# Neighbourhood value matmuls with the whole 128-column chunk stationary

## What is computed

```python
s_loc = jnp.einsum('bqhd,biqjhd->bhqij', q_row, k_win) * scale + jnp.transpose(bias, (0, 2, 1, 3))[None]
s_ctx = jnp.einsum('bqhd,bkhd->bhqk', q_row, k_ctx) * scale
s = jnp.concatenate([s_loc.reshape(B, H, GRID_W, kh * kw), s_ctx], axis=-1)
p = jax.nn.softmax(s.astype(jnp.float32), axis=-1).astype(v.dtype)
out = (jnp.einsum('bhqij,biqjhd->bqhd', p_loc, v_win)
       + jnp.einsum('bhqk,bkhd->bqhd', p[..., kh * kw:], v_ctx))
```

## Time and profile before

| | |
|---|---|
| median of 3 runs | 1832.72 us (1831.17 to 1834.37) |
| the profiled execution's own time | 1831.06 us |
| its span, first to last instruction | 1829.5 us |
| mean granted TensorE clock | 0.968 |
| neighbourhood stage, first transpose of `sc` to the last value matmul | about 1233.4 to 1402 us of the span |

### The profile page before, as it was taken

One profiled execution on the slowest core, in us unless ns is written; L12 is line 12 of the kernel. 1 busy time (PEld: TensorE's weight loads), 2 busy tenths in 40 slices (PEclk: granted clock), 3 DMA queues, 4 the chain that ended last, 5 costly groups with the idle time before them and its releaser, 6 DMA issues.

```text
span 1829.5 us, 23170 instructions
## 1 busy us (share of the span) xinstructions
PE 1733.7 (95%) x9122; PEld 1465.1 (80%) x9122; DVE 981.4 (54%) x1236; ACT 607.0 (33%) x786; POOL 462.5 (25%) x327
## 2 busy tenths in 40 slices
PE   7999999998977799999998999989999899999998
PEld 7888888788866688888887788878777688888887
DVE  4355544756257678355335545427886545434543
ACT  4243432334242222222223233215665333223330
POOL 3000000000019999899600000015663000000000
PEclk8999999999998899999989899988999899999999
DMA  8312134234224334665422112331100323343332
GB/s 256 92 47 70 47 92 138 93 116 161 70 70 138 92 115 147 186 199 173 135 62 86 47 47 70 101 117 31 48 28 24 92 69 92 90 113 84 94 93 77
DMA packets 227579, 178.48 MB, mean 98 GB/s; under 512 B 5971, under 2 KB 217278, under 8 KB 227502
## 3 DMA queue, kind: packets, MB, share of 16 engines
q1 hardware_dynamic: 218206, 142.74, 26.3%
q0 software_dynamic: 8576, 32.23, 5.3%
q10 hardware_dynamic: 720, 2.41, 0.4%
HBM read 171.37 MB, written 9.13 MB: 99 GB/s over the span
## 4 chain that ended last, share of the span: by engine, by line
PE 80%; DVE 7%; POOL 6%; ACT 3%; issue 3%; DMA 1%; DVEq 0%; ACTq 0%; POOLq 0%
PE ps L1374 25%; PE ps L1376 24%; PE ps L1375 24%; DVE w_lo L870 2%; POOL mod_tmp L1846 2%; POOL sc L1911 2%; POOL mod_tmp L1850 1%; PE ps L1511 1%; PE ps L1753 1%; ACT w_hi L530 1%; PE ps L1448 1%; PE ps L1680 1%; POOL mod_tmp L1852 1%; PE ps L1783 1%; ACT vt_h L803 0%
## 5 line engine op out<-in xcount | busy, mean ns | idle before, releaser
L1374 PE MATMUL ps<-h_hi,w_hi 128*128 128x512 f32 x1376 | 543.7, 395 | 16.3 <-DVE h_lo L879 9.7
L1376 PE MATMUL ps<-h_hi,w_lo 128*128 128x512 f32 x1376 | 539.5, 392 | 0.0
L1375 PE MATMUL ps<-h_lo,w_hi 128*128 128x512 f32 x1376 | 539.3, 392 | 0.0
L870 DVE TENSOR_TENSOR w_lo<-w_raw,w_hi 128x2048 fp32r<-128x2048 f32 (+1 forms) x136 | 343.3, 2524 | 109.1 <-ACT w_hi L530 109.0
L1374 PEld LDWEIGHTS ps<-h_hi,w_hi 128*128 128x128 f32 x1376 | 260.9, 190 | 74.3 <-DVE h_lo L879 9.3
L530 ACT ACTIVATE w_hi<-w_raw 128x2048 fp32r<-128x2048 f32 (+1 forms) x136 | 242.5, 1783 | 188.6 <-PE ps L1376 160.6
L1376 PEld LDWEIGHTS ps<-h_hi,w_lo 128*128 128x128 f32 x1376 | 260.4, 189 | 55.6
L1375 PEld LDWEIGHTS ps<-h_lo,w_hi 128*128 128x128 f32 x1376 | 260.7, 189 | 52.6
L1842 POOL DMA_DIRECT2D mod_raw<-in_l_w_mod x24 | 22.0, 916 | 517.8 <-DVE h_lo L879 505.7
L1374 PE MATMUL ps<-a_hi,w_hi 128*128 128x512 f32 x352 | 138.6, 394 | 0.9 <-DVE w_lo L870 0.9
L1375 PE MATMUL ps<-a_lo,w_hi 128*128 128x512 f32 x352 | 138.0, 392 | 0.0
(11 more groups left out here) (284 smaller groups left out, 2789.2 us busy)
## 6 DMA issues: line engine op xcount, KB each, us to landing
mod_raw<-in_l_w_mod POOLq DMA_DIRECT2D x24, 1024.0 KB, 5.8
w_raw<-in_w_ffn_in SPq DMA_DIRECT2D x44, 512.0 KB, 5.1
w_raw<-in_l_ffn_w_up SPq DMA_DIRECT2D x44, 512.0 KB, 4.9
w_raw<-in_w_in SPq DMA_DIRECT2D x40, 512.0 KB, 5.1
w_raw<-in_l_na_w_qkv SPq DMA_DIRECT2D x24, 512.0 KB, 4.5
w_raw<-in_w_mem_kv SPq DMA_DIRECT2D x16, 512.0 KB, 3.9
w_raw<-in_w_ffn_out SPq DMA_DIRECT2D x16, 384.0 KB, 3.5
w_raw<-in_l_ffn_w_down SPq DMA_DIRECT2D x16, 384.0 KB, 3.6
```

The lines of the kernel that those rows point to most:

```text
L870: v.tensor_tensor(wlo[s][:, 0:size], raw[s][:, 0:size], whi[s][:, 0:size].bitcast(F32), ALU.subtract).then_inc(w_lo, 1)
L1374: mm(o, w_h, x_h, start=first, stop=False, **kw)
L1375: mm(o, w_h, x_l, start=False, stop=False, **kw)
L1376: return mm(o, w_l, x_h, start=False, stop=last, **kw)
```

## The change

In `na_values` the slice of the stationary operand to the head's 64 columns is dropped: all 128 columns of the chunk are loaded, and the output is all 128 partitions of bank 6. Each head's product thus also makes 64 partitions that belong to no one (the weights of this head by the values of its neighbour). The two readouts now read the 64 partitions of their own head. The number of instructions, their order and all waits are unchanged.

```diff
@@ na_out on ScalarE, L805
                 rows = slice(64 * half, 64 * half + 64)
                 act.activation(q_hi[rows, at(a), :].rearrange("p o (r t c) -> p (o t) r c", t=4, c=16),
-                               bank(6)[0:64, :].rearrange("p (t r c) -> p t r c", t=4, r=8), ACT.Copy).then_inc(no_hi, 1)
+                               bank(6)[rows, :].rearrange("p (t r c) -> p t r c", t=4, r=8), ACT.Copy).then_inc(no_hi, 1)
@@ na_out on VectorE, L1277
-                                bank(6)[0:64, :].rearrange("p (t r c) -> p t r c", t=4, r=8),
+                                bank(6)[rows, :].rearrange("p (t r c) -> p t r c", t=4, r=8),
@@ na_values on TensorE, L1756
-                a, cols = head // 2, slice(64 * (head % 2), 64 * (head % 2) + 64)
+                a = head // 2
@@
                 for c in range(4):
                     chunk = 2 * tau + c if c < 2 else 6 + c
-                    last = product(bank(6)[0:64, tau * P:tau * P + P], vt_h[a % 2][:, chunk, cols], vt_l[a % 2][:, chunk, cols],
+                    last = product(bank(6)[:, tau * P:tau * P + P], vt_h[a % 2][:, chunk, :], vt_l[a % 2][:, chunk, :],
                                    np_hi[:, g % 2, c * P:c * P + P], np_lo[:, g % 2, c * P:c * P + P], c == 0, c == 3)
```

## The result

| | before | after |
|---|---|---|
| first measurement, median | 1833.55 us (1831.17 to 1834.64, 4 executions) | 1897.33 us (1886.06 to 2009.76, 4 executions) |
| ratio to before | | 1.0329, 95% interval 1.0268 to 1.0390 |
| profiled execution: time, span, mean granted clock | 1831.06, 1829.5, 0.968 | 1891.51, 1889.9, 0.950 |

The change makes the kernel slower by 3.3%, and the time scatters as the one before does not. The ratio leaves out the execution at 2009.76 us; since what moves the executions apart is the very effect at issue, I list all ten that the changed kernel had in the end: 1870.95, 1886.06, 1891.51, 1903.15, 1983.76, 2009.76, 2011.77, 2012.97, 2013.06 and 2013.07 us. Their median is 1996.8 us, 9% above the kernel before, so the 3.3% of the first measurement comes from the quicker ones.

What follows compares the result with a forecast made beforehand. The neighbourhood stage was taken as bound by PE's instruction list with a few waits. Eight pairs at 4.19 us add 33.5 to the median 1832.72, giving 1866.2 us, 1.018 times before; range 1857 to 1877.

Steps and rivals of the forecast that it cites:

- The load sets the distance: Value matmuls: the 128-column weight load outlasts the matmul, distance 0.06 to 0.112 us, each block 0.63 us longer.
- The readouts cost nothing either way: Readouts of L809: the odd heads' changed partitions cost or gain 0, within 3 ns.
- The waits, step by step: One pair's eight steps: part of the block growth falls into present waits, 20.89 to 25.08 us, growth 4.19.
- st = 5: Sixth step of a pair, counted from 0: new 0.42 us readout wait, 2.74 to 3.79 us.
- slack swallowed: Rival on a pair's steps: all present waits used up, no new one, 3.1 us a pair, 1857 us; chance 0.12.
- waits kept: Rival on a pair's steps: waits stay and distances are 0.12, 6.0 us a pair, 1881 us; chance 0.10.
- Eight pairs, 33.5 us: Whole neighbourhood stage: eight pairs of heads at 4.19 us growth each make 33.5 us.
- The edges: Stage's half-clock head, three blocks, -1.6 to +2.0 us, taken as 0; last four steps' growth may shrink, at most 4 times 0.3.
- 2 us of uncertainty: Outside the stage: granted clock may fall or rise some us sooner or later behind the shifted stage, counted as 2 us.
- quick wide load: Rival on the vt_h and vt_l loads: wide as quick as narrow, distance stays 0.06, 1832.7 us; chance 0.04.
- partly hidden one: Rival on the wide load: distance 0.085 us, block grows 0.30, 1.8 us a pair, 1847 us; chance 0.03.

Runs made afterwards that it cites:

- w2_after: Changed kernel plus unread extra matmuls in TensorE's gaps ahead of the stage, 29 in the second gap: 1861.26 to 1866.47 us in four executions, 2011.95 in one.
- w2_before: Kernel before plus unread extra matmuls in TensorE's gaps ahead of the stage, 29 in the second gap: 1829.13 us, 0.9975 of before.
- again_after: Changed kernel run again with no edit: 1870.95, 1983.76 and four times 2012 to 2013 us.
- gap_wide: Changed kernel with narrow loads for the first pair of heads and a TensorE hole made in the fifth pair: 1929.59 to 1936.18 us.
- w_before: Kernel before plus 39 unread matmuls in TensorE's gaps at the head of the stage, 16 in the second gap: 1829.51 us, 0.9979 of before.

## Why the prediction was wrong, point by point

- **The load sets the distance** (0.112 us, block + 0.63). Right. Distances 0.11, block 1.40 against 0.77. Of the parts, the first distance came out shorter than I put down (0.17 us, not 0.22) and the last one, from the last value matmul to the next transposes, longer (0.12, 1345.74 to 1345.86, against 0.05 to 0.06).
- **The readouts cost nothing either way.** Right: the profile after has 590 to 593 ns for L809, in place of 589 to 592.
- **The waits, step by step.** Right. Forecast for the steps of a pair 2.86, 3.33, 6.23, 2.86, 3.79, 3.12 and 2.89, 25.08 in all; measured 2.86, 3.30, 6.18, 2.83, 3.69, 3.07 and 2.82, 24.75, so that a pair grew by 3.86 and not 4.19. The new wait in st = 5 came, and the waits for POOL went, as put down. Both rivals on the waits (slack swallowed, waits kept) are out.
- **Eight pairs, 33.5 us.** Right as the price of the loads, and some 3 us too high: 30.8 us between the stages of w2_after and w2_before, where both keep the full clock, as eight times 3.86 makes it.
- **The edges.** This is the step that failed. I took from the trace of before that "three blocks run in it" and let them cost -1.6 to +2.0 us in all. The bound for one block was sound, 1.2 us against 1.28 measured (2.62 less 1.34 for the narrow one). What was wrong is the number three. The length of the stretch at half clock was copied from a kernel whose blocks stream without a break there, into one whose blocks don't: 13 blocks in the profiled execution, all 64 in again_after's, and the "2 us of uncertainty" for the clock should have been up to 150. The rows to see it by were there: at half clock the narrow distance was 0.11 us, bound by the array, and I wrote that it might double. A doubled distance means an array that idles half of the time in just those blocks that stand where the clock used to come back, and I did not ask what that does to the clock.
- **The other rivals.** The quick wide load and the partly hidden one are out (0.11 us at full clock). The Trainium skill's fast weight load, which "TensorE: Matmul & The Clock Gate", section "Weight-path perf modes — Fast Weight Load (FWL) and DoubleRow", ties to 128 weights of a type that is not FP32, did not appear in `vt_h`'s fp32r loads: median 192 ns, close to the mean of 189 of the 128-column loads in the earlier trace rows.

What stays open: why one execution of w2_after took 2012 us although its gaps ahead of the stage were filled, what it is in the wide blocks that keeps the clock down, and what decides whether the changed kernel's clock comes back after 30, 90 or 360 us. Nor was a kernel tried in which the wide loads have more than 128 moving columns beside them.

Of the versions run, w2_before beats both kernels, if only just: narrow loads and the unread matmuls ahead of the stage, 1829.13 us, 0.9975 of before (0.9959 to 0.9991). The stretch at half clock ahead of the stage is gone in it:

```profile
1225.00:1236.00 11.00, 11.00 (x57) 8.89 (x56) 5.46 (x18) 2.51 (x6) 5.41 (x7) 1.00 0.55 194
```

## What to carry to other kernels

Where few columns move per weight load (128 here), the width of the stationary operand is time: columns that nobody reads cost as much as real ones. When a change makes matmuls load-bound (their distance is set by the weight load and not by the columns that move), ask also what they do at half clock, and whether a stretch at half clock now in the trace still ends. An estimate that takes the length of such a stretch from the kernel before holds only as long as the work in it stays the same.

## What the runs showed of the hardware

- The clock has memory. The same wide blocks ran at full clock for 81 us and at half clock for 153.6 us in one execution, on either side of a 5.75 us hole. The distances of wide and narrow matmuls stand two to one at full clock (0.11 us against 0.06) as at half clock (0.213 against 0.107), and yet the clock stayed at 1.00 for 192.5 us of w2_after: the blocks that did not bring it back did not take it away either. The Trainium skill, "TensorE: Matmul & The Clock Gate", section "HAM oscillation — how this bites in real kernels", describes a clock that is lost again and again in waits of the engine. The runs agree that a wait can take it away (gap_wide, 5.75 us), and go further in what keeps it away: 358.4 us at 0.50 with PE busy 350.87 of them.
- The time of a wide load follows the clock: distances of 0.11 us at full and 0.213 at half clock. The same page's section "LDWEIGHTS (loading the stationary operand)" gives one figure, columns divided by 1.2, in ns, 107 for 128 columns. It fits at full clock; at half clock the measured 213 decides.
- Extra matmuls with no reader can make a kernel faster: 39 of w_before's gave 4 us.
